# Issuing the experts' second-layer weights from ScalarE instead of the sync queue

## The chip, the cores and the metric

One Trainium2 chip, one of its cores. The metric is the device time of one launch in microseconds (us), the median of the runs. Matrix work runs on TensorE (PE, with its weight loads shown as PEld), the element-wise engines are VectorE (DVE), ScalarE (ACT) and GpSimd (POOL), and SyncE (SP) only issues transfers. Transfers that SP issues show in the trace as DMA queue q1, those of ACT as q10, those of POOL as q0; all of them are carried by the same 16 DMA engines.

## The reference, cut to what matters

One layer of a decoder on 1024 tokens of 1024 channels in float32: a mixer (RWKV-7, mLSTM and windowed attention in parallel), then a mixture of experts. The router picks one of 4 groups and 2 of its 8 experts for each token. The part around the change is the expert layer:

```
def expert_block(args):
    xs, e = args                                     # up to 128 routed tokens
    gate, up = jnp.split(xs @ w_e_in[e], 2, axis=-1) # first layer,  1024 x 1024: 4 MB
    return (jax.nn.silu(gate) * up) @ w_e_out[e]     # second layer,  512 x 1024: 2 MB
yb = lax.map(expert_block, (xb, block_exp)).reshape(n_slots, D)
y = jnp.zeros((NT, D), f32).at[slot_tok].add(yb.astype(f32) * slot_w[:, None])
```

There are 32 experts, so 6 MB of float32 weights each and 201 MB in all, and every byte is used once.

## The kernel before

The mixer and the router come first and take about 1374 us of the span. The change touches only the stage behind them, in which the 32 experts are computed one after the other, each on a block of 96 gathered rows.

**Places in memory.** `WE[s][j]` are two sets (s = 0, 1 for even and odd experts) of three places of 2 MB: j = 0 and 1 hold the upper and lower half of an expert's first-layer weights, j = 2 its second-layer weights. A transfer into a place can start when the expert two before has used it.

**TensorE.** `step(e)` computes `first(s, 0)` (96 matmuls over the first half, then `win_half` is raised), turns the activations of expert e - 1 (`hT`), and computes `first(s, 1)` (96 matmuls, then `win_used`). Then come the transposes of the next expert's rows (`xT`) and, after `close` has waited for `wout{s}_in`, `second(1 - s)`, the 96 matmuls of the second layer of expert e - 1, which raise `y`. So the order of use is: first half of e, second half of e, second layer of e - 1. The two halves have semaphores of their own, `win{s}0_in` and `win{s}1_in`.

**SyncE.** `next_weights(e, s, older)` issues the three transfers in just that order, each behind the semaphore of what frees its place: both halves of expert e (line 448), then the second layer of expert e - 1 (line 452) once `y` says that `second` of expert e - 3 is done. All 96 weight transfers are on this one queue.

**VectorE** scales the result of `second` out of PSUM into `e_y[s]` in `y_out` (line 2200), after waiting that the store of two experts before has landed.

**ScalarE** has in a loop of two experts a turn: `hT_out` (line 1584), `silu` (line 1591), `xT_out` (line 1578) and `store`, which waits for `y_out` and issues the two transfers of the expert's rows to memory (lines 1597 and 1598; 288 and 96 KB). It has an `If` for the last turn, which has no next rows.

**GpSimd** gathers the rows of expert e + 2 (line 675, 384 KB) once `xT` of expert e has used their place.

After the last expert the rows of all slots are gathered by token, weighted, added to the residual and stored.

Of the kernel before, what the change touches and what calls it, by code (L numbers as in the profile page):

```python
# [6 lines left out]
P = 128  # L7
# [3 lines left out]
NG, NE, TOPK, DE = 4, 32, 2, 512  # L11
# [10 lines left out]
def hybrid_block(nc, I, out, dram):  # L22
    f32, i32 = mybir.dt.float32, mybir.dt.int32
    ALU, ACT, AX = mybir.AluOpType, mybir.ActivationFunctionType, mybir.AxisListType.X
    ds, ts = bass.ds, bass.ts
# [3 lines left out]
    with ctx:  # L29
# [4 lines left out]
        def sem(name):  # L34
            if name not in sems:
                sems[name] = ctx.enter_context(nc.semaphore(name))
            return sems[name]

        def view(off, *dims):

            n = 1
            for d in dims:
                n *= d
            v = SB[:, off:off + n]
            if len(dims) == 2:
                v = v.rearrange("p (a b) -> p a b", a=dims[0])
            if len(dims) == 3:
                v = v.rearrange("p (a b c) -> p a b c", a=dims[0], b=dims[1])
            return v
# [214 lines left out]
        WE = [[view(12288 * s + 4096 * j, 4, 1024) for j in range(3)] for s in range(2)]  # L264
# [39 lines left out]
        vec_rows, n = [], 0  # L304
# [47 lines left out]
        def _(sp):  # L352
# [94 lines left out]
            def w_in_half(e, s, j):  # L447
                sp.dma_start(WE[s][j], I["w_e_in"][0, ds(e, 1), 512 * j:512 * j + 512, :]
                             .rearrange("a (k p) n -> p (a k) n", p=P)).then_inc(sem(f"win{s}{j}_in"), 16)

            def w_out_of(e, s):
                sp.dma_start(WE[s][2], I["w_e_out"][0, ds(e, 1)]  # L452
                             .rearrange("a (k p) n -> p (a k) n", p=P)).then_inc(sem(f"wout{s}_in"), 16)
# [15 lines left out]
            w_in_half(1, 1, 1)  # L469


            def next_weights(e, s, older):

                sp.wait_ge(sem("win_half"), e - 1)
                w_in_half(e, s, 0)
                sp.wait_ge(sem("win_used"), e - 1)
                w_in_half(e, s, 1)
                if older:
                    sp.wait_ge(sem("y"), 2 * (e - 2))
                w_out_of(e - 1, 1 - s)  # L480

            next_weights(2, 0, False)
            next_weights(3, 1, True)
            with sp.Fori(2, NE // 2) as i:
                for s in range(2):
                    next_weights(2 * i + s, s, True)
            sp.wait_ge(sem("y"), 2 * (NE - 2))
            w_out_of(NE - 1, 1)

            sp.wait_ge(sem("y"), 2 * (NE - 1))  # L490
            for t in range(NT):
# [5 lines left out]
            with sp.If(n_extra > 0):  # L497
                with sp.Fori(0, NX) as j:
                    with sp.If(n_extra > j):
                        e = sp.value_load(i_ex[0:1, ds(j, 1)], min_val=0, max_val=NE - 1)  # L500
# [805 lines left out]
        def _(act):  # L1306
# [268 lines left out]
            def xT_out(e, s):  # L1575
                act.wait_ge(sem("xs_used"), e + 1)
                for k in range(KT):
                    ins = A.activation(e_xT[s][:, k, :], PS[k // 4][:, ts(k % 4, CAP)], ACT.Identity,  # L1578
                                       scale=sc2[:, k:k + 1], bias=sh2[:, k:k + 1])
                ins.then_inc(sem("e_xT"), 1)  # L1580

            def hT_out(e):
                act.wait_ge(sem("hT"), e + 1)
                A.activation(e_hT, PS[2][:, 0:4 * CAP].rearrange("p (k n) -> p k n", k=4), ACT.Copy).then_inc(sem("e_hT"), 1)  # L1584

            def silu(e, first=False):
                act.wait_ge(sem("win_used"), e + 1)
                if not first:
                    act.wait_ge(sem("e_act"), e)
                for r in range(3):  # L1590
                    ins = A.activation(e_g[:, r, :], E_GU[r][:, 0:P], ACT.Silu)  # L1591
                ins.then_inc(sem("e_silu"), 1)

            def store_rows(b, y, stored):

                rows = ys_b[ds(b, 1)].rearrange("o p n -> (o p) n")
                act.dma_start(rows[0:CAP, 0:768], y[0:CAP, :]).then_inc(stored, 16)
                act.dma_start(rows[0:CAP, 768:D].rearrange("(t p) n -> p t n", p=QT),
                              y[CAP:P, :].rearrange("p (t n) -> p t n", t=3)).then_inc(stored, 16)

            def store(e, s):
                act.wait_ge(sem("y_out"), 2 * e + 2)
                store_rows(e, e_y[s], sem(f"y_st{s}"))


            xT_out(0, 0)
            silu(0, True)
# [2 lines left out]
            silu(1)  # L1610
            xT_out(2, 0)
            store(0, 0)
            with act.Fori(1, NE // 2) as i:
                e = 2 * i
                hT_out(e - 1)
                silu(e)
                xT_out(e + 1, 1)
                store(e - 1, 1)
                hT_out(e)
                silu(e + 1)  # L1620
                with act.If(i < NE // 2 - 1):
                    xT_out(e + 2, 0)
                with act.Else():
                    act.nop()
                store(e, 0)
            hT_out(NE - 1)
            store(NE - 1, 1)
            for s in range(2):
# [630 lines left out]
```

## Time and profile before

| | |
|---|---|
| median of 3 runs | 2003.87 us |
| lowest run | 2002.91 us |
| highest run | 2469.56 us |
| time of the profiled execution | 1997.14 us |
| its span, first to last instruction | 1995.4 us |
| busy, PE / PEld | 1839.7 us (92%) / 1028.8 us (52%) |
| busy, DVE / ACT / POOL | 665.5 / 437.6 / 230.5 us |
| mean granted clock of PE | 0.96 |
| DMA, whole span | 334.03 MB, mean 167 GB/s |

Busy is the time in which at least one instruction of the engine ran. Times "from the span's start" are those of the profiled execution. The expert stage lies from 1374 us to 1956 us of the span. A transfer's time "to landing" runs from the start of its issue to its last byte.

### The profile page before, as it was taken

What the parts mean: (1) busy time and instruction counts of PE and PEld (TensorE: products, weight loads), DVE (VectorE), ACT (ScalarE), POOL (GpSimd) and SP (SyncE); (2) the same over time, 40 slices, a digit from 0 to 9 for tenths busy, and PEclk for the clock granted to TensorE, in tenths of its full rate; (3) what the DMA queues carried; (4) which work ended last, traced back from release to release, by engine and by line L of the source; (5) the groups of instructions that cost most, each with busy time, mean ns of one, the idle gap of its engine ahead of it and who ended that gap; (6) DMA issues with size and microseconds to landing.
All of it is one profiled execution on the core that took longest, in us unless ns stands there. A gap on an engine that the chain in (4) does not pass through costs nothing.

```text
span 1995.4 us, 37944 instructions
## 1 busy us (share of the span) xinstructions
PE 1839.7 (92%) x16145; PEld 1028.8 (52%) x16145; DVE 665.5 (33%) x1569; ACT 437.6 (22%) x999; POOL 230.5 (12%) x352
## 2 busy tenths in 40 slices
PE   6999999998998599999999999996999999999990
PEld 3454455554443255555555554554566565665550
DVE  4385344443343532333223333552211111000114
ACT  4220412221223321122121212111222222221210
POOL 3030000000000102221022214001000000000003
PEclk9999999998899799999999999996999999999995
DMA  9386010001112000101010028231999999999988
GB/s 312 110 281 220 11 32 21 21 21 32 42 42 65 17 24 24 30 14 30 17 30 22 21 108 307 108 127 65 388 393 395 392 393 393 390 388 388 388 319 319
DMA packets 146919, 334.03 MB, mean 167 GB/s; under 512 B 19274, under 2 KB 63224, under 8 KB 146844
## 3 DMA queue, kind: packets, MB, share of 16 engines
q1 hardware_dynamic: 127776, 282.68, 39.1%
q0 software_dynamic: 8240, 25.04, 3.8%
q10 hardware_dynamic: 10828, 25.24, 3.2%
q8 instruction: 55, 0.90, 0.2%
q14 instruction: 20, 0.16, 0.0%
HBM read 299.50 MB, written 37.63 MB: 169 GB/s over the span
## 4 chain that ended last, share of the span: by engine, by line
PE 84%; DMA 7%; DVE 3%; ACT 2%; issue 1%; POOL 1%; SPq 1%; ACTq 0%; POOLq 0%; DVEq 0%
PE bank L280 80%; DMA arena<-in_w_e_in 3%; DMA arena<-in_w_in 3%; PE bank L1189 1%; POOL arena L711 1%; PE bank L878 1%; DMA arena<-y_slots,ints 1%; PE bank L1206 1%; PE bank L1128 0%; PE bank L1208 0%; SPq L452 0%; DMA y_slots<-arena 0%; DVE arena L1748 0%; DVE arena L1826 0%; PE bank L754 0%
## 5 line engine op out<-in xcount | busy, mean ns | idle before, releaser
L280 PE MATMUL bank<-arena 128*32 128x256 f32 (+8 forms) x15294 | 1746.8, 380 | 60.2 <-DMA arena<-in_w_in 12.9
L280 PEld LDWEIGHTS bank<-arena 128*32 128x32 f32 (+4 forms) x15294 | 937.8, 134 | 811.3 <-issue 545.6
L2191 DVE TENSOR_TENSOR arena<-arena,bank 128x128 f32<-128x128 f32 x96 | 21.8, 283 | 369.8 <-ACT arena L1591 369.8
L1578 ACT ACTIVATE arena<-bank,arena 128x96 f32<-128x96 f32 x256 | 85.9, 441 | 11.8 <-PE bank L1189 11.8
L675 POOL DMA_INDIRECT arena<-xnorm,ints x32 | 31.6, 987 | 470.9 <-PE bank L1189 450.7
L2200 DVE TENSOR_TENSOR arena<-bank,arena 128x512 f32<-128x512 f32 x64 | 35.7, 558 | 134.6 <-PE bank L280 134.6
L1984 DVE TENSOR_TENSOR arena<-arena,bank 128x256 f32<-128x256 f32 x40 | 16.8, 421 | 172.8 <-PE bank L280 172.8
L626 POOL TENSOR_TENSOR arena<-arena 64x256 f32<-64x256 f32 x96 | 71.1, 741 | 28.7 <-DVE arena L1970 22.0
L1584 ACT ACTIVATE arena<-bank 128x384 f32<-128x384 f32 x32 | 15.7, 490 | 267.7 <-PE bank L1208 267.7
L1529 ACT ACTIVATE arena<-bank 128x256 f32<-128x256 f32 (+1 forms) x48 | 18.4, 382 | 208.7 <-PE bank L280 208.7
L1591 ACT ACTIVATE arena<-bank 128x128 f32<-128x128 f32 x96 | 19.7, 278 | 164.7 <-PE bank L280 164.7
L1711 DVE SCALAR_TENSOR_TENSOR arena<-arena 128x512 f32<-128x512 f32 x70 | 52.7, 752 | 2.5
L1748 DVE RECIPROCAL arena<-arena 128x512 f32<-128x512 f32 x10 | 33.5, 3348 | 33.9 <-ACT arena L1366 33.9
L632 POOL TENSOR_TENSOR arena<-arena 128x512 f32<-128x512 f32 x8 | 10.2, 1272 | 272.6 <-DVE arena L1943 272.6
L1434 ACT ACTIVATE arena<-arena 128x256 f32<-128x256 f32 x64 | 26.4, 494 | 61.9 <-DVE arena L1824 61.9
L1189 PE MATMUL bank<-arena 96*128 96x96 f32 x256 | 28.8, 256 | 5.8 <-DMA arena<-xnorm,ints 5.8
L1943 DVE TENSOR_TENSOR arena<-arena,bank 128x512 f32<-128x512 f32 x32 | 21.9, 683 | 34.4 <-PE bank L280 34.4
L1189 PEld LDWEIGHTS bank<-arena 96*128 96x128 f32 x256 | 22.9, 143 | 18.6 <-issue 18.6
L578 POOL COPY arena<-arena 128x256 f32 (+1 forms) x8 | 3.3, 407 | 248.2 <-PE bank L280 248.2
L570 POOL DMA_DIRECT2D y_slots<-arena x21 | 16.5, 1579 | 125.8 <-PE bank L280 94.8
L1560 ACT ACTIVATE arena<-arena 128x1024 f32<-128x1024 f32 x8 | 8.5, 1056 | 96.4 <-DVE arena L2114 96.4
L1501 ACT ACTIVATE arena<-bank 128x512 f32<-128x512 f32 x32 | 19.1, 596 | 41.4 <-PE bank L280 41.4
(330 smaller groups left out, 1025.5 us busy)
## 6 DMA issues: line engine op xcount, KB each, us to landing
arena<-in_w_e_in SPq DMA_DIRECT2D x64, 2048.0 KB, 21.3
arena<-in_w_e_out SPq DMA_DIRECT2D x32, 2048.0 KB, 21.4
arena<-in_w_ada SPq DMA_DIRECT2D x12, 2048.0 KB, 12.4
arena<-in_w_in SPq DMA_DIRECT2D x32, 512.0 KB, 4.0
y_slots<-arena ACTq DMA_DIRECT2D x32, 288.0 KB, 6.3
y_slots<-arena POOLq DMA_DIRECT2D x21, 384.0 KB, 17.9
arena<-in_x SPq DMA_DIRECT2D x4, 1024.0 KB, 8.4
arena<-in_w_in SPq DMA_DIRECT2D x2, 2048.0 KB, 25.4
```

The source lines that it names most:

```text
L280: return nc.tensor.matmul(o, l, r, start=start, stop=stop)
L626: G.tensor_tensor(a_lo[q][b], a_sm[b, :, 0, b], lvl[b, q, b].unsqueeze(1).to_broadcast([N, H, N]), ALU.mult).then_inc(sem("a_lo"), 1)
L675: pool.indirect_dma_start(out=e_xs[s][0:CAP], out_offset=None, in_=xn_d, in_offset=bass.IndirectOffsetOnAxis(ap=i_ix[s][0:CAP], axis=0), b ...
L711: pool.indirect_dma_start(out=f_y[t % 4][k], out_offset=None, in_=yslot_d, in_offset=bass.IndirectOffsetOnAxis(ap=ix[:, t:t + 1], axis=0))\
L1189: ins = E.transpose(PS[k // 4][:, ts(k % 4, CAP)], e_xs[s][0:CAP, ts(k, P)], ident[0:CAP, 0:CAP])
L1434: A.activation(c_sc[:, j, :], c_sc[:, j, :], ACT.Exp, bias=c_nm[:, j:j + 1])
L1578: ins = A.activation(e_xT[s][:, k, :], PS[k // 4][:, ts(k % 4, CAP)], ACT.Identity, scale=sc2[:, k:k + 1], bias=sh2[:, k:k + 1])
L1711: ins = STT(to, w[:, k, :], cond[:, k:k + 1], to, ALU.mult, ALU.add)
L1748: link(V.reciprocal(c_rs[half], c_rs[half]))
L1943: TT(dst, m_sg[n % 2], PS[7], ALU.mult).then_inc(sem("m_prod"), 1)
L2191: ins = TT(e_h[:, r, :], e_g[:, r, :], E_GU[r][:, P:2 * P], ALU.mult)
L2200: TT(e_y[s][:, cols], PS[5 + u][:, 0:(512, 256)[u]], gt2[:, cols], ALU.mult).then_inc(sem("y_out"), 1)
```

## The change

SP keeps the first-layer halves and the second-layer weights of experts 0 and 1. The second-layer weights of experts 2 to 31 are issued by ScalarE: `w_out_after(e, s)` stands behind `store(e, s)` and loads expert e + 2 into the place that expert e has left. It needs no wait of its own, since `store` has waited for `y_out`, which comes after `second`. The last turn of ScalarE's loop is written out behind the loop (`pair(NE - 2, False)`), which takes the place of the `If`.

```diff
-            def next_weights(e, s, older):
+            def next_weights(e, s):
                 sp.wait_ge(sem("win_half"), e - 1)
                 w_in_half(e, s, 0)
                 sp.wait_ge(sem("win_used"), e - 1)
                 w_in_half(e, s, 1)
-                if older:
-                    sp.wait_ge(sem("y"), 2 * (e - 2))
-                w_out_of(e - 1, 1 - s)
-            next_weights(2, 0, False)
-            next_weights(3, 1, True)
+            next_weights(2, 0)
+            w_out_of(1, 1)
+            next_weights(3, 1)
             with sp.Fori(2, NE // 2) as i:
                 for s in range(2):
-                    next_weights(2 * i + s, s, True)
-            sp.wait_ge(sem("y"), 2 * (NE - 2))
-            w_out_of(NE - 1, 1)
+                    next_weights(2 * i + s, s)
...
+            def w_out_after(e, s):
+                act.dma_start(WE[s][2], I["w_e_out"][0, ds(e + 2, 1)]
+                              .rearrange("a (k p) n -> p (a k) n", p=P)).then_inc(sem(f"wout{s}_in"), 16)
...
             store(0, 0)
-            with act.Fori(1, NE // 2) as i:
-                e = 2 * i
+            w_out_after(0, 0)
+            def pair(e, more):
                 hT_out(e - 1)
                 silu(e)
                 xT_out(e + 1, 1)
                 store(e - 1, 1)
+                w_out_after(e - 1, 1)
                 hT_out(e)
                 silu(e + 1)
-                with act.If(i < NE // 2 - 1):
+                if more:
                     xT_out(e + 2, 0)
-                with act.Else():
-                    act.nop()
                 store(e, 0)
+                if more:
+                    w_out_after(e, 0)
+            with act.Fori(1, NE // 2 - 1) as i:
+                pair(2 * i, True)
+            pair(NE - 2, False)
```

## Rows read from the trace of the kernel before

**Rows 1.** Page, part 2: DMA busy tenths and GB/s, 40 slices of 49.9 us.

```profile
DMA  9386010001112000101010028231999999999988
GB/s 312 110 281 220 11 32 21 21 21 32 42 42 65 17 24 24 30 14 30 17 30 22 21 108 307 108 127 65 388 393 395 392 393 393 390 388 388 388 319 319
```

**Rows 2.** Chain that ended last, in order of time: start us, us, what.

```profile
1816.43 7.41 SPq L452
...
1829.00 28.56 DMA arena<-in_w_e_in
...
1863.19 30.19 DMA arena<-in_w_e_in
```

**Rows 3.** Waits from 1400 to 1948 us: total us, times, longest us.

```profile
PE bank L280 <- DMA arena<-in_w_e_in: 1.9, 3, 0.8
```

**Rows 4.** Timeline of PE, 1852 to 1900 us: start us, us; idle before in brackets.

```profile
1857.60 5.39 PE L280 MATMUL bank<-arena 128*32 128x256 f32 x96 [0.83 <-DMA arena<-in_w_e_in]
...
1875.26 5.39 PE L280 MATMUL bank<-arena 128*32 128x256 f32 x96 [0.25 <-DMA arena<-in_w_e_in]
...
1893.42 5.39 PE L280 MATMUL bank<-arena 128*32 128x256 f32 x96 [0.77 <-DMA arena<-in_w_e_in]
```

**Rows 5.** Timeline of all engines, 1700 to 1724.2 us, one expert's turn.

```profile
1700.76 5.39 PE L280 MATMUL bank<-arena 128*32 128x256 f32 x96
...
1706.89 10.57 PE L280 MATMUL bank<-arena 128*32 128x256 f32 x192
...
1712.47 1.84 SPq L452 DMA_DIRECT2D arena<-in_w_e_out  x1
1712.92 0.32 ACTq L1597 DMA_DIRECT2D y_slots<-arena  x1
1713.40 0.33 ACTq L1598 DMA_DIRECT2D y_slots<-arena  x1
...
1718.08 5.39 PE L280 MATMUL bank<-arena 128*32 128x256 f32 x96
1718.19 0.49 ACT L1584 ACTIVATE arena<-bank 128x384 f32<-128x384 f32 x1 [8.51 <-PE bank L1208]
```

**Rows 6.** Busy times by stretch; the last two columns are DMA share and GB/s.

```profile
1440.00:1613.70 173.70, 173.70 (x3029) 104.29 (x3023) 17.99 (x50) 37.89 (x120) 11.74 (x20) 1.00 1.03 394
1613.70:1787.00 173.30, 173.30 (x3023) 104.02 (x3021) 17.98 (x50) 37.89 (x120) 11.74 (x20) 1.00 1.02 389
...
1720.00:1727.00 7.00, 7.00 (x127) 4.24 (x120) 0.68 (x3) 3.29 (x11) 1.18 (x2) 1.00 1.03 412
1716.00:1719.00 3.00, 3.00 (x54) 1.75 (x50) 0.00 (x0) 0.49 (x1) 0.00 (x0) 1.00 1.03 416
```

**Rows 7.** DMA queues, first 1713 to 1715.9 us (two rows), then 1716.5 to 1718.

```profile
q1 hardware_dynamic: 194, 0.78, 83.4%
q0 software_dynamic: 63, 0.15, 18.3%
...
q1 hardware_dynamic: 101, 0.39, 64.1%
q10 hardware_dynamic: 105, 0.23, 39.0%
```

**Rows 8.** Issues in windows from 1425 and 1706 us: KB each, us to landing.

```profile
arena<-in_w_e_in SPq DMA_DIRECT2D x1, 2048.0 KB, 14.3
...
arena<-in_w_e_in SPq DMA_DIRECT2D x1, 2048.0 KB, 23.2
```

**Rows 9.** Line 452 alone, second-layer weights of experts 28 and 29.

```profile
L452 SPq DMA_DIRECT2D arena<-in_w_e_out x1: 5139/5139/5139, 1872.4 to 1872.4; - x1
...
DMA to landing us min/median/max: 26.3/26.3/26.3
...
L452 SPq DMA_DIRECT2D arena<-in_w_e_out x1: 5157/5157/5157, 1889.9 to 1889.9; - x1
...
DMA to landing us min/median/max: 25.1/25.1/25.1
```

## The prediction

> **What bounds the kernel now.** The first view is the page's DMA rows: up to 1374 us the 16 DMA engines have room, and from the 28th slice on they are full at 388 to 395 GB/s [rows 1]. That is the expert stage, the only one that the change touches; the 1374 us ahead of it keep their time. The second view is one expert's turn [rows 5]: the second-half matmuls start at 1700.76 and again at 1718.08, so a turn is 17.32 us, and TensorE is busy for all of it [rows 6]. The third is the list of waits: on weights TensorE waited three times, 1.9 us in all [rows 3], at 1857.60, 1875.26 and 1893.42, each time in front of the second half of a first layer [rows 4]. So TensorE sets the pace, but only just. An expert moves 6.29 MB of weights, 0.39 MB of gathered rows and 0.39 MB of stored rows, 7.08 MB in 17.32 us or 409 GB/s; the engines gave 394, later 389 [rows 6]. The shortfall of some 17 GB/s makes the transfers later by about 0.7 us an expert. The fourth view shows that: the second half of expert 4, issued at 1429 us, took 14.3 us to land, that of expert 20, issued at 1706 us, 23.2 us [rows 8], 0.56 us more an expert; in the chain at the end it is 28.56 and 30.19 us [rows 2].
>
> The room for this lateness is the same for every weight transfer. A second half's place is free at 1700.76 + 5.39 = 1706.15 and its successor is used two turns after 1700.76, at 1735.40: 29.25 us. For the second layer: `second` ends some 5.3 us after 1706.89, at 1712.2 (the other half of that 10.57 us row is the next first layer), and the place is used again at 1706.89 + 34.64 = 1741.5: 29.3 us. On one queue, served in the order of use, all three transfers of an expert use up this room together, and it runs out only at expert 27, five turns from the end. That order is what the change gives up.
>
> **The change, part by part.**
>
> *Issue on ScalarE.* Thirty instructions more, each some 0.35 us like the stores' 0.32 and 0.33 us. ScalarE has nothing to do from its last store (1713.40 + 0.33) to `hT_out` at 1718.19; its idle time there is 8.51 us [rows 5]. The issue fits into 4.4 us and costs nothing. What is queued behind it is `hT_out`, which `second` needs only behind the next 5.39 us of matmuls and the transposes, so an issue could take 4.4 + 5.4 = 9.8 us before TensorE waits. SyncE's own issues swell to 7.41 us when its queue is long [rows 2, 9], but ScalarE's queue never holds more than one weight transfer and two stores, and its stores took 0.32 us beside SyncE's issue of 1.84 us [rows 5]. Value taken: 0; bounds 0 and, at SyncE's 7.41 us, still 0.
>
> *A later issue.* The second layer is issued at about 1713.8 instead of 1712.47, 1.3 us later, of 29.3 us of room: nothing. The written-out last turn and the missing `If` are sequencer work on an engine that idles: nothing.
>
> *SyncE.* It loses 30 issues. While it hung in them it issued halves late, but these only joined the end of a full queue. No gain, no loss.
>
> *Sharing of the DMA engines.* This is the part with a price. The stores show how two queues share: none of q10's packets stands in 1713 to 1715.9, so its data start 3 us after the issue at 1712.92, and then q10 moves 105 packets against q1's 101, with 23.2 us worth of older work waiting in q1 [rows 7, 8]. The later queue doesn't stand behind the older backlog; the engines take packets of both in turn. Here the weights of both queues are alike 4 KB a row, so I give each half of 400 GB/s. Store and second layer, 0.39 + 2.10 MB, then take 12.5 us plus the 3 us of start: **the second layer lands some 15 to 16 us after its issue at any backlog**, 13 us before it is wanted, and the bytes that it is early by are taken from the halves, which are wanted first.
>
> How much is that at the moment when TensorE waits for the second half of expert e? In the old order everything landed by then was wanted by then. In the new one, the second layer of e - 1 is there in full: 2.10 MB, at 394 GB/s 5.3 us. And that of e has begun: its data start at 1713.8 + 3 = 1716.8 and the half is wanted at 1718.08, 1.3 us at half rate, 0.26 MB or 0.6 us. Together **5.9 us** of lateness that the halves bear alone. Bounds of this term: with fair turns and nothing of e begun, 5.3 us; with the newer queue served first (full rate over 1.3 us), 6.6 us; with no turns at all, 0.
>
> *Where it shows.* Rows of before with 5.9 us added: the room of 29.25 us is used up where the old lateness is 23.3, at expert 20 instead of 27. From there the DMA engines set the pace, a wait of some 0.6 us in front of each second half, as the old kernel has it in its last ones. The end follows from the last such place: the second layer of expert 28 was issued at 1872.4 and landed at 1898.7 [rows 9]; by then, plus 0.6 us, the engines have moved all that the new order moves before the second half of expert 29, which starts at 1899.3 instead of 1893.42, **+5.9 us**. For expert 30 the same reading gives 1889.9 + 25.1 + 0.6 = 1915.6, but TensorE arrives only at 1899.3 + 17.3 = 1916.6 since the gathers have ended: the engines catch up, and the 5.9 us are carried to the end unchanged. None of the old gaps slowed the matmuls behind it (5.39 us for the 96 as ever, [rows 4, 5]), so I add nothing for the clock.
>
> *Total rate.* It decides as much as the order does: 1% of the 490 us from 1400 to 1893 is 4.9 us. With a store beside the halves the engines gave 416 GB/s, alone 412 [rows 6], 1% more; two streams share the engines for 12.5 us of each turn instead of some 3, so at best 1% over half of the time, 2.5 us gained. No row shows two streams of weight reads together. The other end is the drift between the two long stretches, 394 to 389: 1.3%, 6.3 us lost. I take the same rate, 0.
>
> **Sum.** Profiled execution 1997.14 + 0 + 5.9 = 2003.0 us. It lies 6.7 us under the median of the runs shown, a difference as large as the effect, so the effect is put on the median: 2003.87 + 5.9 = 2009.8 us, 0.3% more. A measurement of this kernel can tell about 2% (40 us) from no change, and this is within.
>
> **A rule of the skill.** The rows above say that the queue matters. The Trainium skill, page "DMA: Bandwidth & Descriptors", section "Issuing engines are not separate DMA queues", says that transfers of all issuing engines end on the same 16 DMA engines and interleave, and that issuing from several only saves sequencer time. Read strictly, this edit would move 30 short issues between idle sequencers and the sum would be 2003.9 us; the rows of q1 and q10 agree with the interleaving, but they also show that it lets new work pass old.
>
> **The rivals.**
>
> *Nothing happens, 2003.9 us (0.20).* The bytes are the same and TensorE is the bound for most of the stage. Against it speaks that it needs the new queue to wait behind q1's backlog, or the rate to rise just by what the order loses; a store of 288 KB behind 23 us of backlog did not wait.
>
> *The rate rises, the waits vanish, 2002 us (0.12).* Two queues keep the engines fuller (412 to 416). At 2.5 us gained it gives 2007; only if the engines gave 2% more would the lateness stop growing before it hurts, and then the floor is the old time less the 1.9 us of waits, 2002.0. There is nothing more to gain in the stage, as TensorE is busy without a gap otherwise.
>
> *The rate falls, 2010 + 6.3 = 2016 us (0.13).* Two streams from distant places of memory, at each of the 16 engines in turn.
>
> *ScalarE is held, slower by over 2% (0.02).* If its issue of 2 MB were stretched beyond 9.8 us, as it would be if it had to wait for q1's backlog, `hT_out` would come late and TensorE would wait at `close` in each turn. Each us beyond costs 29 us in all; at 11.2 us it passes 40 us, at 2045. Against it: the longest issue of SyncE, with the full backlog on its own queue, is under 9.8 us in the rows, and ScalarE's were 0.32 us.
>
> The forecast itself (waits from about expert 20 on, +3 to +9 us) has 0.50; 0.03 is left for what I don't see.
>
> **Range.** The low end is the floor less a little scatter of the runs (2002.91 is the lowest), 2001.5; the high end is the falling rate, 2016, with the same allowance, 2017. Faster by over 2%: 0.01, since no more than 1.9 us of waits are there to be removed. Slower by over 2%: 0.03. Within: 0.96.
>
> **What would show it.** Right: second layers on q10 landing in 15 to 16 us throughout; second halves at 17 us already at expert 4 or 5, about 28 to 30 us from expert 20 on; 8 us of waits of TensorE on first-layer weights in ten or more pieces; none on second-layer weights; q1 and q10 moving like numbers of packets; GB/s of the stage at 389 to 394. Wrong: no growth of the halves' landing times over the old ones (the first rival), GB/s above 398 (the second) or under 386 (the third), issues of over 5 us on ScalarE (the fourth). If the first waits appear at expert 20 but their sum isn't 6 us above the old, the term of the total rate is wrong and not that of the order.

## The result and the profile after

The changed kernel takes 2005.1 us (median of 20 runs), the kernel before 1997.36 us (median of 20 runs, the three of the table among them). The medians differ by 7.7 us. The ratio, which leaves out the two runs of the kernel before that took 2469.56 and 3224.58 us, is **1.003, 95% interval 1.0015 to 1.0044**: 6 us slower, 3 to 9, clear of the scatter and far inside 2%. The profiled execution has a span of 2003.8 us against 1995.4.

Of these 8.4 us not all belong to the change. The stage begins 3.7 us later: the issue of the first half of expert 2 stands at 1395.11 instead of 1391.43 us, behind work that is the same in both. I therefore measure within the stage, **from that issue to the start of the second half of expert 29**, the last place where the old kernel waited for weights: 1893.42 - 1391.43 = 502.0 us before [rows 4], 1903.13 - 1395.11 = 508.0 us after.

The timeline of TensorE after, for the rows that had a wait in front (start us, us; the wait in brackets; [rows 4] are those of before):

```profile
1742.32 5.39 PE L280 MATMUL bank<-arena 128*32 128x256 f32 x96 [0.28 <-DMA arena<-in_w_e_in]
...
1760.54 5.39 PE L280 MATMUL bank<-arena 128*32 128x256 f32 x96 [0.82 <-DMA arena<-in_w_e_in]
...
1885.59 5.39 PE L280 MATMUL bank<-arena 128*32 128x256 f32 x96 [0.76 <-DMA arena<-in_w_e_in]
```

and the sum of the waits from 1400 to 1948 us, which answers to [rows 3]:

```profile
PE bank L280 <- DMA arena<-in_w_e_in: 4.4, 9, 0.8
```

The waits begin at 1742.32, which is expert 20, and stand in front of second halves only, as before, but nine times instead of three. A tenth, under the threshold of this list, ends at 1903.13: the chain below shows the transfer that released it. The reason is in the times to landing. The lines of the two issuers, second layers from ScalarE over the stage, then the second half of expert 20:

```profile
L1603 ACTq DMA_DIRECT2D arena<-in_w_e_out x29: 417/418/806, 1425.7 to 1916.3; - x29
...
DMA to landing us min/median/max: 10.4/17.5/18.1
...
L448 SPq DMA_DIRECT2D arena<-in_w_e_in x1: 373/373/373, 1712.9 to 1712.9; - x1
...
DMA to landing us min/median/max: 29.4/29.4/29.4
```

The second layers never need more than 18.1 us, 11 us less than the room they have; the second half of expert 20 needs 29.4 us where it needed 23.2 [rows 8]. In the chain of what ended last every second one of the late turns, from expert 21 to 29, hangs on the transfer of a second half, which spans the two turns between its place becoming free and its use (start us, us, what; compare [rows 2]):

```profile
1837.28 30.12 DMA arena<-in_w_e_in
...
1873.02 30.07 DMA arena<-in_w_e_in
...
1903.13 5.39 PE bank L280 x96
```

The issue on ScalarE costs 0.42 us, and `hT_out` behind it starts with the same idle time in front as in [rows 5], 8.51 us:

```profile
1719.49 0.33 ACTq L1593 DMA_DIRECT2D y_slots<-arena  x1
1719.97 0.33 ACTq L1594 DMA_DIRECT2D y_slots<-arena  x1
1720.45 0.42 ACTq L1603 DMA_DIRECT2D arena<-in_w_e_out  x1
...
1724.75 0.49 ACT L1580 ACTIVATE arena<-bank 128x384 f32<-128x384 f32 x1 [8.51 <-PE bank L1204]
```

The sharpest reading is of bytes. If one kernel waits longer although the engines are full, they have moved something that was not wanted yet. All that the engines moved from the issue of the first half of expert 2 to the start of the second half of expert 29, first before, then after:

```profile
DMA packets 53916, 195.28 MB, mean 389 GB/s; under 512 B 3616, under 2 KB 6259, under 8 KB 53906
```

```profile
DMA packets 54452, 197.49 MB, mean 389 GB/s; under 512 B 3623, under 2 KB 6251, under 8 KB 54442
```

The rate is the same. The new order has moved **2.21 MB more when the same half is there**: one second layer of 2.10 MB and the beginning of the next. At 389 GB/s that is 5.7 us. At one rate the bytes and the time are two views of one quantity; what the bytes add is that the rate is not the cause, since a slower stream would have moved no more.

### The profile page after: what moved, and what is told of

It reads as the page before. It is cut to its first block, busy times and chain, and to the rows that moved or that the text cites. A ratio compares the mean times of both kernels' runs of the same rounds, so it can differ in the third digit from the quotient of the medians.

```text
span 2003.8 us, 37874 instructions
## 1 busy us (share of the span) xinstructions
PE 1846.2 (92%) x16145; PEld 1029.9 (51%) x16145; DVE 665.5 (33%) x1569; ACT 437.8 (22%) x999; POOL 230.7 (12%) x352
## 4 chain that ended last, share of the span: by engine, by line
PE 81%; DMA 11%; DVE 3%; ACT 2%; issue 1%; POOL 1%; ACTq 0%; SPq 0%; POOLq 0%; DVEq 0%
PE bank L280 77%; DMA arena<-in_w_e_in 8%; DMA arena<-in_w_in 3%; PE bank L1185 1%; POOL arena L707 1%; PE bank L874 1%; DMA arena<-y_slots,ints 1%; PE bank L1202 0%; PE bank L1124 0%; DMA y_slots<-arena 0%; DVE arena L1753 0%; PE bank L1204 0%; DVE arena L1831 0%; PE bank L750 0%; ACTq L1312 0%
## 5 line engine op out<-in xcount | busy, mean ns | idle before, releaser
L280 PE MATMUL bank<-arena 128*32 128x256 f32 (+8 forms) x15294 | 1753.1, 380 | 61.7 <-DMA arena<-in_w_in 12.3
```

The costliest lines, as they stand in the source:

```text
L280: return nc.tensor.matmul(o, l, r, start=start, stop=stop)
```

## The experiments

Below, "the interval" is the 502.0 or 508.0 us from the issue of the first half of expert 2 to the start of the second half of expert 29, and "moved" are the bytes of all queues in it. "The order theory" is that the second layer, on a queue of its own, passes the older halves, and that this is the whole cost.

| kernel | profiled execution us | interval us | moved MB | mean GB/s | expert 4 starts at us |
|---|---|---|---|---|---|
| before | 1997.14 | 502.0 | 195.28 | 389 | 66.8 |
| changed | 2005.71 | 508.0 | 197.49 | 389 | 69.6 |
| changed, again | 2006.23 | 505.3 | 197.40 | 391 | 66.8 |
| only the loop written out | 2000.50 | 502.7 | 195.66 | 389 | 69.6 |
| each transfer on both queues | 2003.77 | 508.0 | 198.17 | 390 | 70.0 |
| late issue | 2011.88 | 513.1 | 196.56 | 383 | 69.6 |
| late issue from expert 15 on | 2006.87 | 507.1 | 196.31 | 387 | 66.8 |
| only even experts on ScalarE | 2007.77 | 506.8 | 197.41 | 390 | 68.4 |
| only odd experts on ScalarE | 2006.61 | 506.8 | 197.29 | 389 | 66.8 |
| all weights on ScalarE | 2009.93 | 506.3 | 196.66 | 388 | 70.4 |
| half of the second layer's rows, changed | 1993.36 | 499.9 | 171.59 | 343 | 66.8 |
| half of the second layer's rows, before | 1995.71 | 499.9 | 171.70 | 343 | 66.8 |
| before, with a useless load | 2029.74 | 535.3 | 209.10 | 391 | 66.8 |
| changed, with a useless load | 2042.10 | 540.6 | 211.15 | 391 | 66.8 |

The bytes speak of the order only where TensorE waits for the second half of expert 29. It doesn't wait there with half of the second layer's rows (twice), with only the loop written out and with all weights on ScalarE. With only the odd experts on ScalarE it last waits one turn earlier, and with each transfer on both queues it waits for second layers. In these rows the engines may be ahead of TensorE, and the bytes contain that lead. Experiments 4 to 12 are one run each, so they are read within the stage; the second column holds the part ahead of it too, which scatters by more than 10 us.

The last column is the start of the second half of expert 4, from the same origin. It differs for two reasons. In some profiles TensorE's granted clock was lower in the first turns, whatever the kernel: in the changed kernel TensorE waited 2.82 us for `xT_out` near 1401 us, and the clock stood at 0.50, the lower of its two levels (1.2 and 2.4 GHz), from 1404 to 1408 us; after a wait of the same length it stayed at 1.00 in experiment 12. Over the first 40 us that makes 0.91 against 1.00. And in the kernels with first-layer weights on ScalarE (experiments 2 and 11) that engine waits for `win_used` ahead of its `xT_out`, and TensorE waited there 4.3 us instead of 2.8.

**1. Only ScalarE's loop is written out.**

```diff
-            with act.Fori(1, NE // 2) as i:      # with an If for the last turn
+            with act.Fori(1, NE // 2 - 1) as i:
+                pair(2 * i, True)
+            pair(NE - 2, False)                  # no w_out_after anywhere, SyncE as before
```

> All weights on SyncE's queue as before, only ScalarE's loop is written out for the last turn as in the changed kernel. I measure from the issue of the first half of expert 2 to the start of the second half of expert 29: 502.0 us before, 508.0 us after the change. Order theory (the second layer on its own queue passes the older halves): 502.0, ratio 1.000 to the kernel before. Rival, that the new program text of ScalarE costs something: part of the 6 us or of the 3.7 us by which the stage began later in the profile after (1395.1 instead of 1391.4 us), a ratio of 1.002.

Ratio 1.0009, interval 0.9983 to 1.0035. TensorE never waited for weights: it had started 2.8 us later in its first turns, ran 25 turns of 17.33 us and was at expert 29 at 502.7 us, 1.6 us behind the landing of the half (1896.5 us). The ratio alone would not decide, as its interval overlaps that of the change. What decides is that the changed kernel's first profile, with the same late start, has ten waits on weights and is 5.3 us longer within the stage. The stage began at 1395.4 us here too, but between 1389.7 and 1401.1 us in the other profiles, the 1389.7 in a kernel with the new text of both engines; so this is scatter of the part ahead of the stage and not the text.

**2. Each transfer cut in two, one part on each queue, in the old order.**

```diff
-    sp.dma_start(WE[s][j], ...)                     # 2 MB on SyncE
+    sp.dma_start(WE[s][j][:, 0:2], ...)             # 1 MB on SyncE
+    act.dma_start(WE[s][j][:, 2:4], ...)            # 1 MB on ScalarE, same moment
```

> Every weight transfer of experts 2 to 31 is cut in two of 1 MB, one on each queue, issued in the order of use: ScalarE now issues 90 transfers. Order theory: with the order kept on both queues the second layer cannot pass the halves, 502 us from the first half of expert 2 to the second half of expert 29, second halves landing at 14 us for expert 4 and 23 us for expert 20 as before, ratio 1.000. Rival, that two streams side by side or ScalarE's issuing cost the time: 508 us or more, ratio 1.003 or more. Rival, that two streams raise the rate: under 500.5 us and no waits.

This missed: ratio 1.0046 (1.0019 to 1.0073), 508.0 us. Here are the two parts of the second half of expert 16, both issued at 1640.6 us:

```profile
L449 SPq DMA_DIRECT2D arena<-in_w_e_in x1: 373/373/373, 1640.6 to 1640.6; - x1
...
DMA to landing us min/median/max: 10.2/10.2/10.2
...
L1609 ACTq DMA_DIRECT2D arena<-in_w_e_in x1: 469/469/469, 1640.6 to 1640.6; - x1
...
DMA to landing us min/median/max: 23.5/23.5/23.5
```

The order was kept on each queue, not between them. ScalarE's queue carries the stores as well, 3.54 MB a turn against 3.15; the engines serve both by turns, so SyncE's parts are there at once and **the backlog collects on the queue with more to carry** (medians over the interval 9.6 us to landing on SyncE's queue, 19.9 and 23.8 us on ScalarE's). TensorE needs both parts and waits for the later one, here seven times on second layers, 5.6 us. It is the same mechanism as in the change (2.89 MB more are moved at the place of comparison), brought in by the experiment itself, so as a test of "two queues without passing" it decides nothing.

**3. and 4. The second layer issued later, so that less of it is early.**

```diff
                 silu(e)
+                w_out_after(e - 2, 0)
...
                 store(e - 1, 1)
-                w_out_after(e - 1, 1)
                 hT_out(e)
                 silu(e + 1)
+                w_out_after(e - 1, 1)
```

> The changed kernel, with the second-layer issue moved behind silu of the next turn, some 10.5 us later, still on ScalarE's queue. Order theory: by the time TensorE wants the second half of an expert, its queue neighbour has had 8.0 us at some 172 GB/s (1.38 MB, 3.5 us of all engines) instead of 2.10 MB, nothing of the next one, and a store of 0.28 MB less (0.7 us): 2.8 us of lateness instead of 5.9, so 504.8 us from the first half of expert 2 to the second half of expert 29. Rival, that the number of queues or the issuing engine costs: 508 us as in the changed kernel; if the later issue hurts instead, waits on second-layer weights and over 508 us.

It was slower still: ratio 1.0086 (1.0052 to 1.0119), 513.1 us. But the bytes moved too early fell as the order theory says, from 2.21 to 196.56 - 195.28 = 1.28 MB (1.1 expected, 2.8 us at 390 GB/s). What grew besides is the time in which the engines had nothing to do. The first 40 us and the next 120 us of the stage with the late issue (last column GB/s):

```profile
1394.44:1434.44 40.00, 37.17 (x604) 22.04 (x596) 12.71 (x67) 7.60 (x24) 2.35 (x4) 0.91 0.90 326
1434.44:1554.44 120.00, 120.00 (x2098) 72.06 (x2094) 12.59 (x35) 26.61 (x84) 8.25 (x14) 1.00 1.02 388
```

and of the kernel before:

```profile
1391.43:1431.43 40.00, 37.18 (x647) 23.01 (x643) 13.39 (x70) 9.85 (x33) 3.12 (x5) 1.00 0.99 368
1431.43:1551.43 120.00, 120.00 (x2098) 72.03 (x2094) 12.42 (x35) 25.24 (x82) 7.46 (x14) 1.00 1.03 395
```

326 instead of 368 GB/s over 40 us are 1.7 MB, 388 instead of 395 over 120 us 0.8 MB: 6.4 us that the engines don't get back, because later on they are the narrow place. Part of this is TensorE's lower clock in the first turns of this profile; against the first profile of the changed kernel, which had the same 0.91 (362 and 392 GB/s), it is 1.9 MB or 4.9 us. To see whether that is all, the issue is late only from expert 15 on, when there is a backlog.

> The changed kernel up to expert 14, and from the second layer of expert 15 on the issue 10.5 us later, behind silu, as in the run with the late issue. That run took 513.1 us where 504.8 was expected; in its first 40 us the engines moved 326 GB/s instead of 368, in the next 120 us 388 instead of 395, as there was nothing to do for them while the second layer was held back: 2.5 MB or 6.4 us. If that is the reason, the late issue from expert 15 on, with a backlog to work on, gives the 504.8 us of the order theory, under the 508.0 of the changed kernel. Rival, that a late issue costs in itself (stores behind the weights on ScalarE's queue, the rate): 508 to 511 us.

507.1 us, and 1.03 MB too early. The start of the stage is cured, 6.0 us of the late issue's loss are gone, some of them with the clock, which was not low here; the byte term is again the expected one, half of the change's. But I expected 504.8 us: 2.3 us are missing, and they are in the rate, 387 GB/s over the interval instead of 389. Why the engines move 0.5% less with the late issue is open; its gathers land in 8.6 us (median) instead of 7.6. With 2.3 us missing the rival of the expectation, a late issue that costs in itself, is not excluded. Behind the interval both kernels with a late issue also wait 2.15 us for the second layer of expert 31, where the kernel before and the changed one wait 1.49 and 1.22 us for `hT_out`; this is part of the late issue's ratio.

**5. and 6. Half of the second-layer rows: a load under the rate of the engines.**

```diff
-    act.dma_start(WE[s][2], I["w_e_out"][0, ds(e + 2, 1)] ...
+    act.dma_start(WE[s][2][:, 0:2], I["w_e_out"][0, ds(e + 2, 1), 0:2 * P] ...
```

> The changed kernel with only 256 of the 512 rows of the second-layer weights loaded for experts 2 to 31 (the other rows stay those of experts 0 and 1, so the result differs). 6.03 MB a turn, 348 GB/s, is under what the engines give. Order theory: no lateness builds up, no waits of TensorE on weights, second halves landing at a constant 9 to 11 us, 500 us from the first half of expert 2 to the second half of expert 29 and a turn of 17.32 us. Rival, that issuing on ScalarE costs something in each turn: a turn above 17.32 us here too, 0.2 us or 5 us in all.

> The kernel before with only 256 of the 512 rows of the second-layer weights loaded for experts 2 to 31 (the result differs). Both theories: 500 us from the first half of expert 2 to the second half of expert 29, no waits on weights, the same as the changed kernel with half of the rows within 0.5 us if the order theory holds and the load is under the rate.

From the second half of expert 4 to that of expert 29 it is 1889.65 - 1456.49 = 433.16 us with the issue on ScalarE and 1892.90 - 1459.73 = 433.17 us with that on SyncE, 25 turns of 17.33 us; no waits on weights in either, and with the issue on ScalarE the halves land in 9.2 to 12.3 us near 1710 us. Timeline of TensorE with the issue on ScalarE:

```profile
1456.49 0.85 PE L280 MATMUL bank<-arena 128*32 128x256 f32 x12
...
1889.65 0.64 PE L280 MATMUL bank<-arena 128*32 128x256 f32 x8
```

**The issue on ScalarE costs nothing here**, and the passing costs nothing either as long as there is no backlog to pass.

**7. and 8. A useless load of 0.52 MB more in each turn.**

```diff
                 w_in_half(e, s, 1)
+                sp.wait_ge(sem("small_in"), 16 * len(smalls) + 16 * (e - 3))
+                sp.dma_start(view(30720, 1, 1024), I["w_e_in"][0, ds(e - 1, 1), 0:P, :] ...
```

> The kernel before with a useless load of 0.52 MB more behind the second half of experts 4 to 31, on SyncE's queue: 7.60 MB a turn, at 392 GB/s a turn of 19.4 us. All theories: the waits on the second halves begin near expert 11 and the whole is 30 to 40 us longer than before.

> The changed kernel with the same useless load. Order theory: the lateness that the halves bear is one second layer (5.3 us) and what has begun of the next (0.6 to 1.5 us), whatever the load: against the kernel before with this load the second half of an expert starts 6 to 7 us later once both are bound by the engines, and the same at expert 29 as at expert 15. Rival, that two queues lower the rate of the engines: a difference that grows by 0.2 to 0.3 us in each turn from expert 10 to 29, 4 to 6 us more at the end than at expert 15.

Both kernels wait for weights from expert 11 on, the changed one from expert 8. From the common origin the changed one starts the second half of expert 11 5.5 us later than the other, of expert 15 5.3 (271.8 against 266.5), of expert 20 5.6, of expert 25 4.9, of expert 29 5.2 us (540.6 against 535.3). The difference is there once and does not grow over 18 turns: it is a shift of the order, not a rate and not a cost of each turn. It is 1 us smaller than I wrote, one second layer (5.3 us) and nothing of the next; 211.15 - 209.10 = 2.05 MB says the same. In the changed one two rows of 96 matmuls took 7.07 and 7.06 us instead of 5.39, right behind waits of 1.49 and 1.50 us, with the granted clock at 0.51 from 1651.6 to 1655 us behind the second of these waits; the difference to the other kernel did not grow by it, since the engines set the pace.

**9. and 10. Only the even, only the odd experts on ScalarE.**

> Only the second layers of even experts are issued by ScalarE, those of odd experts by SyncE in the old order. I measure again from the issue of the first half of expert 2 to the start of the second half of expert 29 (502.0 us before, 508.0 after). Order theory: what counts is the one second layer that is there too early when the last waiting half lands; for expert 29 that is the one of expert 28, on ScalarE's queue: 5.3 us, so 507.3 us. Rival, a cost in each turn that adds up (a lower rate, an issue): half the issues, half the cost, 505.0 us.

> Only the second layers of odd experts are issued by ScalarE. Order theory: expert 29's second half has nothing too early beside it (the one of expert 28 stands behind it in SyncE's queue), but expert 28's has that of expert 27: it starts 5.5 us later than before, TensorE then runs a turn of 17.33 us, and the second half of expert 29 starts at 506.6 us. Waits on the second halves of even experts alone. Rival, a cost in each turn: 505.0 us.

506.8 us in both (507.3 and 506.6 expected, 505.0 by the rival). These times alone don't decide, since two profiles of one kernel can lie some 3 us apart (experiment 12). The bytes do, which scatter by 0.1 MB only: with the even experts, where TensorE waits for the half of expert 29, 197.41 - 195.28 = 2.13 MB more, the whole second layer and not half of it. And the waits stand where the theory puts them. Odd experts on ScalarE, three of TensorE's six waits:

```profile
1815.54 5.39 PE L280 MATMUL bank<-arena 128*32 128x256 f32 x96 [1.25 <-DMA arena<-in_w_e_in]
...
1850.95 5.39 PE L280 MATMUL bank<-arena 128*32 128x256 f32 x96 [0.69 <-DMA arena<-in_w_e_in]
...
1886.99 5.39 PE L280 MATMUL bank<-arena 128*32 128x256 f32 x96 [1.31 <-DMA arena<-in_w_e_in]
```

Even experts on ScalarE, two of five:

```profile
1869.07 5.39 PE L280 MATMUL bank<-arena 128*32 128x256 f32 x96 [1.26 <-DMA arena<-in_w_e_in]
...
1905.01 5.39 PE L280 MATMUL bank<-arena 128*32 128x256 f32 x96 [1.22 <-DMA arena<-in_w_e_in]
```

All waits are some 36 us apart, two turns, in the one on even experts alone (here 24, 26 and 28) and in the other on odd ones alone (here 27 and 29): at each expert behind the one whose second layer has passed.

**11. All weights on ScalarE, in the order of use.**

```diff
+            def in_after(e, s, j):
+                act.wait_ge(sem(("win_half", "win_used")[j]), e + 1)
+                act.dma_start(WE[s][j], I["w_e_in"][0, ds(e + 2, 1), ...
```

> All weights of experts 2 to 31 but one second layer are issued by ScalarE, in the order of use, on its queue; SyncE's queue is empty. Order theory: one queue in the old order, so nothing passes anything and the lateness grows as before; 502 to 504 us as long as ScalarE is not held. Rival, that ScalarE's queue or its issuing is what costs: 508 us or more already from the middle of the stage on. A third effect can come on top: SyncE's issues swelled to 5 to 9 us from expert 21 on; three of these in a turn are more than the 13 us that ScalarE has idle, so the last turns may get longer, with TensorE waiting on ScalarE and not on weights.

No wait of TensorE on weights at all: on one queue in the order of use nothing passes. The turns stay at 17.33 us up to expert 26. Then ScalarE is held in its own issues; timeline of both engines:

```profile
1852.42 5.12 ACTq L1597 DMA_DIRECT2D arena<-in_w_e_in  x1
...
1858.21 3.80 ACTq L1597 DMA_DIRECT2D arena<-in_w_e_in  x1
...
1865.35 5.39 PE L280 MATMUL bank<-arena 128*32 128x256 f32 x96 [1.20 <-ACT arena L1562]
```

The two issues of 5.12 and 3.80 us push `xT_out` (here line 1562) behind the end of the matmuls before, 1.20 us, and again two turns later (0.81 us; a third stop, 0.39 us, lies behind the interval). With its late first turns (70.4 instead of 66.8 us) and 25 turns of 17.33 us it would be at expert 29 at 503.6 us; the other 2.7 us to 506.3 were lost in the last three turns, 2.0 of them in these two stops. Not 502 to 504, but for the third reason that the expectation names and not for the rival's.

**12. The changed kernel once more.**

> The changed kernel once more, unchanged, for how far one profile can be trusted. The stage begins anywhere between 1390 and 1401 us in the profiles so far, and the second half of expert 4 starts 66.8 or up to 70.8 us after the issue of the first half of expert 2, by the clock in the first turns. If the DMA engines set the end of the stage, as the order theory has it, neither matters: 508.0 us from the first half of expert 2 to the second half of expert 29, within 0.5 us. Rival, that the 508.0 contain the late start of TensorE in that profile: 505 to 511 us, moving with expert 4.

505.3 us: outside of my half microsecond. Bytes and places agree with the first profile (197.40 against 197.49 MB; ten waits, 4.6 us in all), the rate doesn't, 391 against 389 GB/s. The first 40 us, in the first profile and in this one:

```profile
1395.11:1435.11 40.00, 37.18 (x604) 21.94 (x596) 12.73 (x67) 7.58 (x24) 2.36 (x4) 0.91 0.97 362
...
1399.10:1439.10 40.00, 37.18 (x647) 23.05 (x643) 13.40 (x70) 9.85 (x33) 3.11 (x5) 1.00 0.99 368
```

In the first profile the lower clock in the first turns made the requests come later: 362 GB/s in the first 40 us, here 368 as in the kernel before, 0.24 MB or 0.6 us. In the next 120 us it is 392 against 395, another 0.36 MB or 0.9 us, but experiment 1 with its clock of 0.91 has 394 there, so this part is not shown to be the clock's; the rest is spread over the stage and open. So the interval has a scatter of about 3 us, the bytes one of 0.1 MB. Like starts are best set against each other: the first profile is 5.3 us longer than experiment 1 (both 69.6 in the last column). Set against the profile of before with an equally early start, the change costs 505.3 - 502.0 = 3.3 us: 2.12 MB more (5.4 us) at a rate 0.4% higher (2.1 us back).

## Why the prediction was right, and where it failed

**The base failed.** The text says "so the effect is put on the median: 2003.87 + 5.9 = 2009.8". The effect holds, +0.3% foretold and 1.003 (1.0015 to 1.0044) measured, but 2003.87 was the median of three runs and 6.5 us above the 1997.36 of twenty. The run at 2469.56 is not to blame: the other two, 2002.91 and 2003.87, are themselves among the four highest of the eighteen that the ratio uses. Set against 1997.36, the forecast 2009.8 stands for a change of 12.4 us or 0.6%, twice the measured 0.3%; the wrong step is as large as the effect. The profiled execution, 1997.14 us, which the same paragraph sets aside, would have given 1997.14 + 5.9 = 2003.0, against 2005.1 measured; but that a single run lay so near the median is luck, as the eighteen spread from 1991 to 2004. The time lies within the range, 2001.5 to 2017, and within 2%.

**The term of the order was right.** 2.36 MB too early (2.10 and 0.26) were written, 2.21 and 2.12 MB measured; 5.9 us against 5.7 and 5.4. The full second layer is there; of the 0.26 MB of the next one only 0.11 and 0.02 are. The runs with a useless load, with even, and with odd experts alone carry it: a shift by one second layer, there once, wherever it is allowed to pass.

**The place was right.** Waits from expert 20 on, in front of second halves, none on second layers. Their sum was not: 8 us foretold, 4.4 and 4.6 measured. In the first profile TensorE had lost 2.9 us in its first turns already, which the weights made use of; in the second the rate was 0.4% higher. Counted from turn to turn, the delay between expert 4 and expert 29 is 3.1 and 3.3 us above that of the kernel before.

**Early landing times were wrong.** The second half of expert 4 was to take 17 us; it took 11.3 in the first profile, in which TensorE's first requests came 2.9 us late, and 14.6 in the second, against 14.3 before [rows 8]. The second layers take 17.5 us where I had 15 to 16; the share of half the rate that I gave them is too high (below). It was read from numbers of packets, 105 and 101; by bytes the store had 0.23 of 0.62 MB in the same two rows [rows 7], 37%, and the second layer has 31 to 41% in the stretches below. This changes nothing in the sum, since at the place that counts the second layer of e - 1 is there in full either way.

**ScalarE was right:** 0.42 us an issue, nothing behind it late, shown free by the pair with half of the rows. The rival in which it is held was seen with three weight issues in a turn, in the last turns of experiment 11, and not with one.

**The rate was right as a range, not as a number.** "I take the same rate, 0": 389, 389 and 391 GB/s. Its term moved by 2 us between two profiles of one kernel, a third of the effect; the 2% more that the second rival needs was in no interval. For a stretch it was there, but in another kernel: experiment 2, with like parts on both queues, had 399 GB/s from 1671.8 to 1791.8 us, where the kernel before has 388. Why is open.

**The rule.** The Trainium skill, page "DMA: Bandwidth & Descriptors", section "Issuing engines are not separate DMA queues", says first that transfers from all issuers end on the same engines and interleave. The trace agrees: 324 packets of q1 and 176 of q10 within the same 5 us (below). It says second that only sequencer time is saved. Where the engines were under their rate the issuer indeed made no difference, 433.17 and 433.16 us. By my sum this second half would have given 2003.9 us, 0 us of effect, and it fails here, ratio 1.003 (1.0015 to 1.0044), where the engines are full and deadlines differ: the queue decides what passes what. That 2003.9 lies nearer to the measured 2005.1 than 2009.8 does is the wrong base again and speaks for no rule.

**A reading was off by one slice:** the engines are full from the 29th slice on, which begins at 1397 us, and not from the 28th, which has 65 GB/s [rows 1]. Nothing in the sum rests on it.

That the cost is the passing and not ScalarE or its text is shown by experiments 1 and 5 to 8, by the bytes and the places of the waits in 9 and 10, and by the absence of weight waits in 11. That the whole of the 6 us (3 to 9) of the twenty runs is this term is argued: the profiles give 3.3 and 6.0 us, and 5.3 between profiles with a like start. The direct cross-check, SyncE alone issuing the second layer ahead of the halves, was not run. No version that beats the kernel before was found; its own waits for weights are 1.9 us.

## What to carry to other kernels

When the DMA engines are full, one queue served in the order of use is a schedule, and a second queue is a way past it: what comes early there does so at the expense of everything else. Look for the transfer with the least room to spare, and count the bytes that will be in memory when it lands and are not wanted yet; divided by the rate that is about the price, once, not per turn (here 5.2 to 5.7 us foretold by the bytes, 3.3 to 6.0 seen in time). Take the base of a small forecast from many runs: with three, or with one profiled execution, the base can be off by as much as the effect.

## What the runs showed of the hardware

**Two queues with like transfers did not share evenly.** In the changed kernel, with nothing but weights on the two queues (halves on q1, a second layer on q10, in pieces of some 4 KB), from 1746 to 1751 us, then from 1838 to 1842 us:

```profile
q1 hardware_dynamic: 324, 1.29, 67.8%
q10 hardware_dynamic: 176, 0.72, 35.8%
...
q1 hardware_dynamic: 282, 1.12, 70.2%
q10 hardware_dynamic: 125, 0.51, 32.1%
```

From 1834 to 1838 us it was 243 to 173 packets. So the first queue had 1.4 to 2.3 times the packets of the second; what sets the share is not settled.

**A gather slows a full stream.** In the kernel before the engines gave 326 GB/s from 1713.2 to 1716 us, with the packets of a gather (q0) beside q1's, and 412 GB/s from 1720 to 1727 us [rows 6].

**A lost start is not made good.** With the late issue the engines had moved 2.5 MB less than in the kernel before after 160 us of the stage, and 2.9 MB less after 480 us (183.94 against 186.87 MB).

**An issue takes longer the more its own queue has outstanding, on either engine.** 0.42 us with one second layer and two stores on ScalarE's queue, 3.8 and 5.1 us with all weights on it; SyncE's three issues of halves between 1865 and 1885 us (1863 and 1883 us in the kernel before) take 0.37 us each in the changed kernel, with the second layers gone from its queue, and 4.6 to 9.0 us before.
